# A second place for the experts' down weights, filled ahead of gate/up and copied on chip

## The reference, cut to what matters

```python
def expert_block(args):
    xb, e = args
    gu = xb @ w_gu[e] + b_gu[e]                     # 1024 x 2048 per expert
    gate = jnp.minimum(gu[:, :D_EXPERT], SWIGLU_LIMIT)
    up = jnp.clip(gu[:, D_EXPERT:], -SWIGLU_LIMIT, SWIGLU_LIMIT)
    glu = gate * jax.nn.sigmoid(SWIGLU_ALPHA * gate)
    return ((up + 1.0) * glu) @ w_down[e] + b_down[e]   # 1024 x 1024 per expert
```

## Time and profile before

| | us |
|---|---|
| three runs | 2097.85, 2089.7, 2097.7; median 2097.7 |
| the profiled execution, its own time | 2097.68 |
| its span, first to last instruction | 2095.9 |
| PE busy / PE weight loads busy | 2003.0 (96%) / 1303.3 (62%) |
| DVE busy / ACT busy | 906.1 (43%) / 642.1 (31%) |
| weight queue's share of the 16 DMA engines | 71.4%, 579 MB |
| granted TensorE clock, mean | 0.986 of full speed |

### The profile page before, as it was taken

One profiled execution on the slowest core, in us unless ns is written; L12 is line 12 of the kernel. 1 busy time (PEld: TensorE's weight loads), 2 busy tenths in 40 slices (PEclk: granted clock), 3 DMA queues, 4 the chain that ended last, 5 costly groups with the idle time before them and its releaser, 6 DMA issues.

```text
span 2095.9 us, 31088 instructions
## 1 busy us (share of the span) xinstructions
PE 2003.0 (96%) x12274; PEld 1303.3 (62%) x12275; DVE 906.1 (43%) x1591; ACT 642.1 (31%) x972; POOL 56.3 (3%) x65
## 2 busy tenths in 40 slices
PE   6998999989999999999999999999999999999999
PEld 4864333323333333333333598889999999799999
DVE  2523122112211221122122367876885549776874
ACT  1422111111111111111111335544664344634653
POOL 0000000000000000000000220000000020000000
PEclk9997999999999999999999999999999999999999
DMA  9785999469999999999999564324564644235553
GB/s 338 280 326 228 423 426 425 183 253 425 426 426 427 428 425 425 426 428 426 425 384 427 205 181 141 121 81 144 179 199 144 184 131 141 81 121 161 183 190 111
DMA packets 186466, 580.51 MB, mean 277 GB/s; under 512 B 21472, under 2 KB 138976, under 8 KB 150400
## 3 DMA queue, kind: packets, MB, share of 16 engines
q1 hardware_dynamic: 186368, 579.08, 71.4%
HBM read 577.74 MB, written 1.31 MB: 276 GB/s over the span
## 4 chain that ended last, share of the span: by engine, by line
PE 72%; DMA 20%; DVE 4%; ACT 2%; issue 1%; SPq 0%; ACTq 0%; DVEq 0%
DMA ring<-in_w_gu 17%; PE bank L1096 15%; PE bank L1104 7%; PE bank L1361 3%; PE bank L817 3%; PE bank L1594 3%; PE bank L1362 3%; PE bank L1363 3%; PE bank L1596 3%; PE bank L1595 3%; PE bank L887 2%; PE bank L1042 2%; PE bank L1056 2%; DMA ring<-in_w_in 2%; PE bank L1610 2%; PE bank L1612 1%
## 5 line engine op out<-in xcount | busy, mean ns | idle before, releaser
L1096 PE MATMUL bank<-ring,heap 128*64 128x512 f32 x2112 | 474.2, 601 | 24.1 <-DMA ring<-in_w_gu 24.1
L1096 PEld LDWEIGHTS bank<-ring,heap 128*64 128x64 f32 x2112 | 146.4, 138 | 330.1 <-issue 281.7
L2249 DVE TENSOR_SCALAR heap<-bank 128x256 f32<-128x256 f32 x66 | 25.0, 420 | 685.3 <-PE bank L1096 685.3
L1104 PE MATMUL bank<-ring,heap 128*64 128x512 f32 x1120 | 249.5, 596 | 0.3 <-DVE heap L2306 0.3
L1747 ACT ACT_TABLE_LOAD x32 | 41.1, 1283 | 500.7 <-DVE heap L2249 500.7
L1594 PE MATMUL bank<-h_hi,w_hi 128*128 128x256 f32 x640 | 182.4, 285 | 4.6 <-DVE w_lo L2576 4.6
L2576 DVE TENSOR_TENSOR w_lo<-ring,w_hi 128x2048 fp32r<-128x2048 f32 (+1 forms) x64 | 142.4, 2226 | 102.5 <-ACT w_hi L1953 102.5
L1361 PE MATMUL bank<-h_hi,w_hi 128*128 128x256 f32 x640 | 185.0, 289 | 1.2 <-DVE w_lo L2381 1.2
L1362 PE MATMUL bank<-h_lo,w_hi 128*128 128x256 f32 x640 | 182.1, 284 | 0.0
L1363 PE MATMUL bank<-h_hi,w_lo 128*128 128x256 f32 x640 | 181.9, 284 | 0.0
L1595 PE MATMUL bank<-h_lo,w_hi 128*128 128x256 f32 x640 | 181.8, 284 | 0.0
(11 more groups left out here) (361 smaller groups left out, 2989.1 us busy)
## 6 DMA issues: line engine op xcount, KB each, us to landing
ring<-in_w_gu SPq DMA_DIRECT2D x128, 2048.0 KB, 20.1
ring<-in_w_down SPq DMA_DIRECT2D x128, 1024.0 KB, 19.0
ring<-in_ffn_w_up SPq DMA_DIRECT2D x44, 1024.0 KB, 7.7
ring<-in_w_in SPq DMA_DIRECT2D x32, 1024.0 KB, 7.9
ring<-in_w_ada SPq DMA_DIRECT2D x24, 1024.0 KB, 10.4
ring<-in_ffn_w_down SPq DMA_DIRECT2D x16, 1024.0 KB, 5.7
ring<-in_w_out SPq DMA_DIRECT2D x8, 1024.0 KB, 5.0
ring<-in_w_in SPq DMA_DIRECT2D x3, 2048.0 KB, 26.9
```

The source lines that it names most:

```text
L1096: last = mm(psum[g][both[f], :], gu_input(xgT, k), wt[:, g, f, :], start=False, stop=k == DT - 1, skip_group_check=True)
L1104: last = mm(psum[bank][FEW * f:FEW * f + n, :], x[:, o:o + n], wt[:, 512 * f:512 * (f + 1)], start=k == 0, stop=k == DT - 1)
```

## The change

The down weights get a second place, `staged`, 4 pieces of 2,048 words in the heap (4 MB in all). From expert 1 on, SP loads a down piece there, and DVE (dn0, dn1) and ACT (dn2, dn3) copy it into the ring once PE is through with the old piece. PE then waits for the copy (`moved`) and not for the transfer. On the queue, the down weights of expert 1 come before all of expert 0's; then for each e the queue has gu0 to gu3 of expert e+1 and after them the down pieces of expert e+2, each of which waits until the copy of expert e+1's piece has emptied its place.

```diff
+STAGE = HEAP - TT * 320 - 4 * UNIT
+BIAS = STAGE - 2 * 512 - 2 * FEW
...
+            def load_staged(e, j):
+                sp.dma_start(staged[j], down_rows(e)[:, j // 2, j % 2, :]).then_inc(stage_in[j].sem, 16)
...
             exp_names = [name for name, _ in EXPERT]
+            last_of("s7")
+            for j in range(4):
+                load_staged(1, j)
             load_expert(0, after_mixer, exp_names[0:2] + exp_names[4:8] + exp_names[2:4])
-            with sp.Fori(0, NE - 1) as e:
-                load_expert(e + 1, after_expert(e), exp_names)
+            with sp.Fori(0, NE - 2) as e:
+                load_expert(e + 1, after_expert(e), exp_names[0:4])
+                for j in range(4):
+                    by = moved["dve" if j < 2 else "act"]
+                    sp.wait_ge(by.sem, by.at(j % 2 + 1, e + 1))
+                    load_staged(e + 2, j)
+            load_expert(NE - 1, after_expert(NE - 2), exp_names[0:4])
...
+            def down_arrived(e, j):
+                by = moved["dve" if j < 2 else "act"]
+                pe.wait_ge(by.sem, by.at(j % 2 + 1, e))
...
-                        pe.wait_ge(exp_in[f"dn{k // 2}"].sem, exp_in[f"dn{k // 2}"].at(16, e))
+                        down_arrived(e, k // 2)
...
             with act.Fori(0, NE) as e:
                 by_count(act, e, expert)
+                with act.If(e < NE - 1):
+                    for j in (2, 3):
+                        act.wait_ge(stage_in[j].sem, stage_in[j].at(16, e))
+                        if j == 2:
+                            act.wait_ge(dn_used.sem, dn_used.at(3, e))
+                        else:
+                            act.wait_ge(y_full.sem, y_full.at(R, e))
+                        f(piece(exp_stream, f"dn{j}", 1)[:, 0, :], staged[j], ACT.Copy).then_inc(moved["act"].sem, 1)
...
             with dve.Fori(0, NE) as e:
                 by_count(dve, e, expert)
+                with dve.If(e < NE - 1):
+                    for j in (0, 1):
+                        dve.wait_ge(stage_in[j].sem, stage_in[j].at(16, e))
+                        dve.wait_ge(dn_used.sem, dn_used.at(j + 1, e))
+                        v.tensor_copy(piece(exp_stream, f"dn{j}", 1)[:, 0, :], staged[j]).then_inc(moved["dve"].sem, 1)
```

More of the change, by code:

```diff
@@ L273, in build @@
         f_hi, f_lo = sb("f_hi", [P, FT, T], F32R), sb("f_lo", [P, FT, T], F32R)
-        sb("between", [P, 16384 - LRING])
+        sb("between", [P, RING + BIAS - LRING - SPLIT])
         bias_pair = sb("bias_pair", [P, 2, 512], F32R)
@@ L364, in build @@
         scale1, scale2 = take(8), take(8)
+        vtok = take(TT, P)
+        decay, decay2 = take(4), take(4)
+        small_done = take(1)
+        mod_rows = take(512)
+        w_rg = take(2 * 4, 64)
+        small = take(64)
+        stat = take(8, 2, NH)
+        attnT = take(4, T)
+        w_route = take(DT, NE)
+        b_down = take(D)[0:NE, :]
+        probs = take(NH, 384)
+        pT = take(2, 384)
+        assert take.areas[0][1] <= STAGE, take.areas
+        take = Carve()
+        take.areas[0][1:] = [STAGE, STAGE + 4 * UNIT]
         qT = take(4, T)
         kT = take(2, T)
-        vtok = take(TT, P)
         xr = take(4, 3 + T)
@@ L372, in build @@
         lru_t = take(4, T)
[L373 to L384, removed]
         xn = sq
@@ L390, in build @@
         sq_lru, sq_attn = lru_t, hT[:, 0:4, :]
-        sq_x1 = heap[:, 7500:7500 + DT * T].rearrange("p (a b) -> p a b", a=DT)
+        sq_x1 = flat_probs[:, 0:DT * T].rearrange("p (a b) -> p a b", a=DT)
         bias_cols = qT.rearrange("p a b -> p (a b)")[:, 0:512]
-        bias_raw = lru_a.rearrange("p a b -> p (a b)").rearrange("p (a b) -> p a b", a=2)
+        bias_raw = hT[:, 4:8, :].rearrange("p a b -> p (a b)").rearrange("p (a b) -> p a b", a=2)
         logits = attnT[0:NE, 0, :]
@@ L434, in build @@
         xgT = take_e(4, 2, FEW)
-        act_g, act_u, act_s = take_e(512), take_e(512), take_e(512)
-        hid, hidT, y_sb = take_e(512), take_e(512), take_e(512)
+        hidT, y_sb = take_e(512), take_e(512)
         sg_both = take_e(2 * T)
         sgT, sgC = sg_both[:, 0:T], sg_both[:, T:2 * T]
+        act_g, act_u, act_s = take_e(512), take_e(512), take_e(512)
         xgC = take_e(4, 2, FEWER)
-        act_gc, act_uc, act_sc, hid_c, hidT_c = take_e(T), take_e(T), take_e(T), take_e(T), take_e(T)
-        y_c = take_e(512)
+        act_gc, act_uc, act_sc = take_e(T), take_e(T), take_e(T)
+        hid, hid_c, hidT_c = act_u, act_uc, act_gc
+        y_c = x_tok
         pick, pickg = take_e(TT, T), take_e(TT, 2 * T)
         gateT = take_e(T)
-        expert_end = take_e.areas[0][1]
+        assert take_e.areas[0][1] <= BIAS, take_e.areas
+        staged = [heap[:, STAGE + UNIT * j:STAGE + UNIT * (j + 1)] for j in range(4)]
         router_at = HEAP - TT * 320
-        assert expert_end <= router_at, (expert_end, router_at)
         router = heap[:, router_at:HEAP].rearrange("p (a b) -> p a b", a=TT)
@@ L455, in build @@
         gu_used, dn_used = signal("gu_used", GU - 1), signal("dn_used", 3)
+        stage_in = [signal(f"stage_in{j}", 16) for j in range(4)]
+        moved = {"dve": signal("moved_by_dve", 2), "act": signal("moved_by_act", 2)}
         x_full, x_ready = signal("x_full", R), signal("x_ready", R)
@@ L680, in _, with down_rows @@
                              bias_rows.rearrange("e (b f n) -> f e b n", b=2, f=2)[g % 2]).then_inc(bias_in.sem, 16)
+            def down_rows(e):
+                return dram["w_down"][e].rearrange("(f c p b) n -> p c f (b n)", f=2, c=2, b=2)
+            def load_staged(e, j):
+                sp.dma_start(staged[j], down_rows(e)[:, j // 2, j % 2, :]).then_inc(stage_in[j].sem, 16)
             def load_expert(e, free, names):
                 gu = dram["w_gu"][e].rearrange("(q p b) n -> p q (b n)", p=P, b=2)
-                dn = dram["w_down"][e].rearrange("(f c p b) n -> p c f (b n)", f=2, c=2, b=2)
+                dn = down_rows(e)
                 for name in names:
@@ L700, in free @@
                     j = int(name[2])
-                    if name.startswith("gu"):
-                        return (gu_used.sem, gu_used.at(j + 1, e)) if j < GU - 1 else (up_full.sem, up_full.at(R, e))
-                    return (dn_used.sem, dn_used.at(j + 1, e)) if j < 3 else (y_full.sem, y_full.at(R, e))
+                    return (gu_used.sem, gu_used.at(j + 1, e)) if j < GU - 1 else (up_full.sem, up_full.at(R, e))
                 return free
             exp_names = [name for name, _ in EXPERT]
+            last_of("s7")
+            for j in range(4):
+                load_staged(1, j)
             load_expert(0, after_mixer, exp_names[0:2] + exp_names[4:8] + exp_names[2:4])
-            with sp.Fori(0, NE - 1) as e:
-                load_expert(e + 1, after_expert(e), exp_names)
+            with sp.Fori(0, NE - 2) as e:
[5 more added lines that the diff above has]
+            load_expert(NE - 1, after_expert(NE - 2), exp_names[0:4])
             if stop == "moe":
@@ L1257, in double @@
                     if r == 0:
-                        pe.wait_ge(exp_in[f"dn{j}"].sem, exp_in[f"dn{j}"].at(16, e))
+                        down_arrived(e, j)
                     for k in (2 * j, 2 * j + 1):
@@ L1803, in _ @@
             act.wait_ge(slots_ready.sem, 2)
+            for j in (2, 3):
+                act.wait_ge(exp_in[f"dn{j}"].sem, 16)
+            f(router[:, 0, 62:63], router[:, 0, 60:61], ACT.Copy).then_inc(moved["act"].sem, 2)
             with act.Fori(0, NE) as e:
                 by_count(act, e, expert)
+                with act.If(e < NE - 1):
+                    for j in (2, 3):
+                        act.wait_ge(stage_in[j].sem, stage_in[j].at(16, e))
[4 more added lines that the diff above has]
+                        f(piece(exp_stream, f"dn{j}", 1)[:, 0, :], staged[j], ACT.Copy).then_inc(moved["act"].sem, 1)
             for i in range(4):
@@ L2318, in expert @@
                 select_bias(e + 1).then_inc(sel_ready.sem, 1)
+            for j in (0, 1):
+                dve.wait_ge(exp_in[f"dn{j}"].sem, 16)
+            v.tensor_copy(router[:, 0, 61:62], gsum[:, 0, 0:1]).then_inc(moved["dve"].sem, 2)
             with dve.Fori(0, NE) as e:
                 by_count(dve, e, expert)
+                with dve.If(e < NE - 1):
+                    for j in (0, 1):
+                        dve.wait_ge(stage_in[j].sem, stage_in[j].at(16, e))
+                        dve.wait_ge(dn_used.sem, dn_used.at(j + 1, e))
+                        v.tensor_copy(piece(exp_stream, f"dn{j}", 1)[:, 0, :], staged[j]).then_inc(moved["dve"].sem, 1)
             dve.wait_ge(route_in.sem, 48)
```

## The result

The change makes the kernel slower. The median of four runs is 2228.6 us (2225.6 to 2234.7), that of the kernel before on the same chip 2096.1 us, the ratio 1.0641 with a 95% interval of 1.0624 to 1.0657. The profiled execution took 2234.7 us around a span of 2232.9, which is 137.0 us more than the span of before.

The account below looks back on a forecast made before the run. The prediction took DMA to bound experts 13 to 26 at 29.52 us each, and PE the other experts. Its terms, 2.3 + 1.8 = 4.1 us on 2097.7, gave 2101.8 us, range 2087.5 to 2108.

Parts of the forecast that it names:

- rival B: ACT's loop: the added branch makes it too long, so each expert fetches code; about 195 us slower, 2293, chance 0.09.
- the period in the long stream: DMA-bound experts 13 to 26: 29.5 us per expert; the prediction called itself wrong if this changed at all.
- decides from two: ACT has 8.2 us to spare per expert, so one code-fetch idle is hidden and two, 15.5 us, cost time.
- The order of the stream, 0 us: DMA queue: the extra room gives a down lead of one expert, nothing to gate/up, which PE waits for: 0 us.
- Rival A: DMA queue: the second place stores 4 MB more, so the stream starts 9.84 us ahead: 2087.9 us, chance 0.13.
- The queue's wait for the copies, +2.3: From expert 7: down pieces wait for copies to empty their places; the stream slips once, +2.3 us, ends 0.7 and 3.
- The `double` of 27, +1.8: Expert 27's two passes: ACT's down copies delay its copy of gathered rows, on PE's path: +1.8 us, ends 0 and 2.
- Rival C: Weight stream: DMA stands still for one copy of four, 1.9 us in each of 19 experts: +36 us, 2134, chance 0.08.

Follow-up runs that it names:

- the one with 96 in front: The changed kernel with 96 one-column writes added ahead of VectorE's first instruction: 2100.2 us, ratio 1.0020.

## Why the prediction was wrong

**The outcome** was rival B, with a chance of 0.09, in kind: instruction packets between 600 and 1000 us, idles ended by "issue", slower. The forecast of 2101.8 and the range to 2108 missed, and the prediction's own sign of being wrong, that the period in the long stream changes at all, came true: 34.4 us for 29.5.

**The step that failed** is the dismissal of B: "the loops loop today without one, and the block is short". Both halves are true and say nothing of the room that is left. So the sum had code fetch at nothing, where it costs 4.9 us per expert and some 130 in all. DVE's loop had room for 4 to 8 instructions; the added branch moved its end from 442 to 451, past the edge. The rival itself was wrong in two points. It named ACT; the fetches are DVE's, and 400 more instructions on ACT cost nothing. And it priced the engine's own idle, of which one per expert was to be hidden, so it "decides from two". With 16 never-executed writes DVE idles 365 us and with the copies 200, at the same time of the whole; the price is 0.98 us per packet on the one DMA engine that also carries weights, five times per expert. With that price B would have come to an estimated 31 x 4.9 = 152 us, less what the DMA makes up while it has room, as in slices 7 and 8, where it came to 195; measured are 132.

**The order of the stream, 0 us: right.** In the four versions of the change that fetch no code in the loop and keep the copies split, the first bound expert is still 13 and the time is 0.15 to 0.26% above the kernel before. Rival A is refuted: the 31 us that the run without down weights shows are not reached by a place for down.

**The queue's wait for the copies, +2.3: too large, about 1 measured.** From the start of expert 7 to the turn of the rows in the `double` of 27, four kernels that fetch nothing and have no copies take 583.0 to 583.2 us (before: 1028.89 − 445.73). Of the four with the split copies three take 0.9 to 1.1 us more, the one with 96 in front the same as these, so the slip is not there each time. (The prediction's own working is also off by a little: 470.8 + 9.84 is 480.6 and not 480.8, which makes 2.4.) DVE's copy takes 1.23 us, not 2.2; the Trainium skill's rule for float32 copies (VectorE: DVE Perf Modes, Mode 2×_2P), an estimated 1.07, was the nearer one. And no table load stands ahead of ACT's copies (1.90 us each, 3.70 for both). These rows are of the kernel with DVE's body emptied:

```profile
1025.94 0.60 ACT L1789 ACTIVATE heap<-bank 128x512 f32<-128x512 f32 x1 [6.43 <-PE bank L1128]
1026.43 3.70 ACT L1840 ACTIVATE ring<-heap 128x2048 f32<-128x2048 f32 x2
1030.17 1.28 ACT L1766 ACT_TABLE_LOAD   x1
1031.46 0.60 ACT L1766 ACTIVATE heap<-bank 128x512 f32<-128x512 f32 x1
```

**The `double` of 27, +1.8: nothing measured.** In the same kernel the copies end at 1030.13 and PE's gathered rows are ready at 1030.08, so ACT does its load and copy as early as before. PE waits 0.32 us as before, 22.69 us behind the group of expert 26 (1032.12 − 1009.43) for 22.68 (1028.89 − 1006.21). The term failed by the 1.28 us of a table load and the 0.3 us of a branch that it put ahead of the copies: from the start of ACT's result copy to the end of both copies are 4.2 us, not 6.0.

```profile
1029.91 1.89 PE L1120 MATMUL bank<-ring,heap 128*64 128x512 f32 x8
1032.12 0.74 PE L1069 MATMUL bank<-consts_sb,heap 128*128 128x128 f32 x4 [0.32 <-ACT heap L1766]
```

**Not foreseen, +2.0:** as PE changes bodies before expert 7 it idles 9.7 to 10.3 us in the kernel after and all five built from it, and 7.5 to 8.0 us in the kernel before and all seven built from that, the padded ones too. The number of PE's code packets (q8) is the same, seven from 400 to 480 us, in before, after and the four versions that keep the split. Why they take longer is open. So the sum for the change without its fetches was 4.1, and the four versions give 2.0 to 4.3 by the medians. That these agree is luck: the parts are other ones than in the sum, about 1 for 2.3, 0 for 1.8, and 2.0 that it did not have.

**Rival C: refuted**, by 426 GB/s with all copies running.

**No version beats the kernel before.** The best with the change, its tail placed once, is 0.15% slower.

## What to carry to other kernels

Before code is added inside a loop, look whether the profile shows instruction packets in the loop's steady part, and treat "none" as a state that a few instructions can end, also instructions that never run and instructions in front of the loop. If such packets appear, price them against the DMA stream, not against the engine that fetches: a stream that is the bound pays for its slowest DMA engine. A second buffer gives a lead only to the piece that the bound waits for; ask the chain of waits which one that is.

## What the runs showed of the hardware that was not expected

- A code packet of 8 KB costs the DMA engine that it rides on 0.98 us: 0.325 for itself, and 1.273 instead of 0.61 for the 16 KB data packet behind it (median over some 75 of 101 code packets from 400 to 1150 us). Packets that take 0.3% of the DMA's share in the long stream, 0.2% by the page, cost 6.4% of the kernel's time.
- Twelve one-column writes, run once ahead of the loop, made a kernel of 2096 us one of 2226; sixteen did not.
- What is never executed counts by where it puts the code behind it: 16 and 400 instructions cost the same on DVE (2227.5 and 2230.0 us), 400 on ACT nothing (2094.6).
- A float32 copy of 128x2048 within SBUF took 1.23 us on DVE and 1.90 on ACT, and both beside the DMA's full rate of 426 GB/s.
